# Layer 1's masked-decay products in column tiles of 32 token rows, and the cumulated decays kept in DRAM by steps, in a two-layer GLA and SSD decoder step

## The reference

```python
def ssd_chunk_step(S, inp):
    x, dt, a, Bm, Cm = inp
    c = x.shape[1]
    acum = jnp.cumsum(a, axis=1)
    causal = jnp.tril(jnp.ones((c, c), dtype=bool))[None, :, :, None, None]
    lmat = jnp.exp(jnp.where(causal, acum[:, :, None] - acum[:, None], -jnp.inf))
    cb = jnp.einsum('bign,bjgn->bijg', Cm, Bm)
    y = jnp.einsum('bijg,bijgr,bjgrp->bigrp', cb, lmat * dt[:, None], x)
    y = y + jnp.einsum('bign,bgrpn->bigrp', Cm, S) * jnp.exp(acum)[..., None]
    a_last = acum[:, -1]
    w = jnp.exp(a_last[:, None] - acum) * dt
    S = jnp.exp(a_last)[..., None, None] * S + jnp.einsum('bjgn,bjgr,bjgrp->bgrpn', Bm, w, x)
    return S, y
```

## Time and profile before

| | |
|---|---|
| median of 3 runs | 1575.83 us (1575.52 to 1580.14) |
| the profiled execution | 1581.91 us, of which the trace spans 1580.2 us |
| TensorE, matmuls | 1474.9 us busy, 93% of the span |
| TensorE, weight loads | 1232.4 us busy, 78% (beside the matmuls) |
| VectorE | 1176.9 us, 74% |
| ScalarE | 824.1 us, 52% |
| GpSimd | 252.0 us, 16% |
| mean granted TensorE clock | 0.973 of full speed |
| DMA | 242.92 MB, mean 154 GB/s |

### The profile page before, as it was taken

One profiled execution on the slowest core, in us unless ns is written; L12 is line 12 of the kernel. 1 busy time (PEld: TensorE's weight loads), 2 busy tenths in 40 slices (PEclk: granted clock), 3 DMA queues, 4 the chain that ended last, 5 costly groups with the idle time before them and its releaser, 6 DMA issues. The chain is left out here.

```text
span 1580.2 us, 28320 instructions
## 1 busy us (share of the span) xinstructions
PE 1474.9 (93%) x10074; PEld 1232.4 (78%) x10074; DVE 1176.9 (74%) x2595; ACT 824.1 (52%) x1837; POOL 252.0 (16%) x438
## 2 busy tenths in 40 slices
PE   6989999799999969998999999989989999999985
PEld 5969787567788759898888888867777788888764
DVE  4555587856786887967887898986869787687775
ACT  4735353445556545546665664644646364654451
POOL 5010113001331200111120121210002110000012
PEclk8999999999999999999999999999999999999988
DMA  6455455434576433448855865853675775666641
GB/s 188 134 146 145 138 154 165 119 120 138 145 185 189 141 118 105 142 112 212 236 139 128 234 172 133 232 125 86 194 198 144 177 183 141 171 147 154 163 134 60
DMA packets 312198, 242.92 MB, mean 154 GB/s; under 512 B 32808, under 2 KB 283500, under 8 KB 311900
## 3 DMA queue, kind: packets, MB, share of 16 engines
q1 hardware_dynamic: 302140, 208.28, 48.9%
q0 software_dynamic: 9920, 32.84, 7.7%
HBM read 180.40 MB, written 64.97 MB: 155 GB/s over the span
## 5 line engine op out<-in xcount | busy, mean ns | idle before, releaser
L1439 PE MATMUL bank<-h,w 128*128 128x268 f32 (+1 forms) x4752 | 842.8, 332 | 27.0 <-ACT w L857 21.4
L1439 PEld LDWEIGHTS bank<-h,w 128*128 128x128 f32 x4752 | 706.8, 193 | 104.9 <-issue 33.1
L873 DVE TENSOR_TENSOR w<-w_raw,w 128x1024 fp32r<-128x1024 f32 x132 | 161.0, 1220 | 40.1 <-ACT w L857 39.5
L842 PE MATMUL bank<-s_w_out,s_yt_hi 128*128 128x512 f32 (+2 forms) x544 | 169.7, 402 | 3.2 <-DVE s_ys L2522 2.5
L857 ACT ACTIVATE w<-w_raw 128x1024 fp32r<-128x1024 f32 x132 | 138.7, 1051 | 14.1 <-DMA w_raw<-in_ssd_w_in_dram 14.1
L1517 DVE SCALAR_TENSOR_TENSOR conv<-before_conv,cw,conv 128x260 f32<-128x260 f32 (+2 forms) x216 | 125.3, 580 | 4.2
L842 PEld LDWEIGHTS bank<-s_w_out,s_yt_hi 128*128 128x128 f32 (+2 forms) x544 | 97.1, 182 | 30.5 <-issue 4.2
L842 PE MATMUL bank<-g_w_out,g_ot_hi 128*128 128x512 f32 (+2 forms) x288 | 95.7, 421 | 1.1 <-DVE g_ot_lo L2065 0.9
L842 PE MATMUL bank<-s_w_out,s_yt_lo 128*128 128x512 f32 x240 | 95.6, 398 | 0.0
L2311 ACT ACTIVATE s_decay<-s_decay,t_ac 128x128 f32<-128x128 f32 (+1 forms) x288 | 85.4, 379 | 1.2
L1485 ACT ACTIVATE conv<-bank,cw 128x268 f32<-128x268 f32 (+1 forms) x72 | 45.9, 637 | 75.5 <-PE bank L1439 59.9
(11 more groups left out here) (256 smaller groups left out, 2491.2 us busy)
## 6 DMA issues: line engine op xcount, KB each, us to landing
w_raw<-in_ssd_w_in_dram SPq DMA_DIRECT2D x80, 512.0 KB, 4.2
w_raw<-in_gla_w_in_dram SPq DMA_DIRECT2D x48, 512.0 KB, 4.3
s_decay<-kept_acd SPq DMA_DIRECT2D x32, 512.0 KB, 8.1
w_raw<-in_ssd_w_out_dram SPq DMA_DIRECT2D x30, 512.0 KB, 4.4
g_chunk<-kept_gq SPq DMA_DIRECT2D x32, 448.0 KB, 4.9
s_chunk<-kept_sq SPq DMA_DIRECT2D x32, 384.0 KB, 4.8
kept_sq<-stage SPq DMA_DIRECT2D x80, 134.0 KB, 4.4
kept_sq<-stage SPq DMA_DIRECT2D x40, 256.0 KB, 4.6
```

The source lines that it names most:

```text
L842: last = pe.matmul(bank[0:r, :], yt[a][:, k, 0:r], wo[:, b, 512 * half:512 * half + 512], start=(k + a + b == 0), stop=(k == tiles - 1 and ...
L873: dve.tensor_tensor(self.part(i, 1), self.raw(i), hi, ALU.subtract).then_inc(self.w_lo, 1)
L1439: last = pe.matmul(bank[:, 0:n], w[:, p.tile % 2, a, k, :], h[:, b, k, c:c + n], start=(i == 0), stop=(i == len(terms) - 1))
```

## The change

Three things are edited.

1. In `pe_scan` the product of one head is split over its output's token rows into column tiles of 32: four matmuls with a 128x32 stationary operand, each with its output in another quarter of the PSUM partitions. The moving operand is the same 128x64 slice for all four. Steps of 24 tokens keep one matmul for a head.
2. `kept_acd` is laid out as steps x heads x 128 tokens instead of heads x all tokens. The load of a step's decays reads 8 neighbouring rows of 128, which are 4 KB without a gap, and its DMA is written with 128 rows of 1024 elements instead of 128x8x128.
3. The store of group 0's decays is two DMAs (step 0 with 24 tokens, steps 1 to 4 with 128) instead of one. `all_stored` waits for the higher count.

```diff
-    for name, shape in (("gq", [U, 7 * P, T]), ("sq", [U, 10 * P, T]), ("acd", [SH, T]), ("meta_rows", [NM, D]),
+    for name, shape in (("gq", [U, 7 * P, T]), ("sq", [U, 10 * P, T]), ("acd", [STEPS, SH, P]), ("meta_rows", [NM, D]),
...
     def store(self, sp, G):
         sp.wait_ge(self.scanned, G + 1)
-        c, n = GROUP_COL[G], GROUP_LEN[G]
-        sp.dma_start(self.d["acd"][:, c:c + n], self.room(G)[2]).then_inc(self.stored, 16)
+        ac, q = self.room(G)[2], GROUP_STEPS[G]
+        if G == 0:
+            sp.dma_start(self.d["acd"][0, :, 0:C0], ac[:, 0:C0]).then_inc(self.stored, 16)
+            ac, q = ac[:, C0:], q[1:]
+        sp.dma_start(self.d["acd"][q[0]:q[-1] + 1].rearrange("s h c -> h s c"),
+                     ac.rearrange("h (s c) -> h s c", c=P)).then_inc(self.stored, 16)
+
+    def all_stored(self, engine, G):
+
+        engine.wait_ge(self.stored, 16 * (G + 2))
...
-            sp.wait_ge(self.sizes.stored, 16 * (G + 1))
+            self.sizes.all_stored(sp, G)
...
-        sp.dma_start(self.decay(u, s), d["acd"][HPG * u:HPG * u + HPG, c:c + n].unsqueeze(0).to_broadcast(
+        sp.dma_start(self.decay(u, s), d["acd"][s, HPG * u:HPG * u + HPG, 0:n].unsqueeze(0).to_broadcast(
             [P, HPG, n])).then_inc(self.acb_in[e % 2], 16)
...
         for r in range(HPG):
-            last = pe.matmul(self.Y[0][0:n, r * HD:(r + 1) * HD], G[0:n, r, :], t["xdt"][0:n, r * HD:(r + 1) * HD],
-                             start=True, stop=True)
+            for j in range(0, n, SUB):
+                rows = slice(j, min(j + SUB, n))
+                last = pe.matmul(self.Y[0][rows, r * HD:(r + 1) * HD], G[0:n, r, rows],
+                                 t["xdt"][0:n, r * HD:(r + 1) * HD], start=True, stop=True)
         last.then_inc(self.intra, 1)
...
-            act.wait_ge(self.sizes.stored, 16 * (group_of(s) + 1))
+            self.sizes.all_stored(act, group_of(s))
```

## The result

The changed kernel takes 1552.45 us (median of 4 runs, 1551.42 to 1553.76), the kernel before took 1577.99 us beside it (4 runs, 1575.52 to 1583.47). The ratio is 0.9834, with a 95% interval of 0.9804 to 0.9864: 26 us less, between 21 and 31. The forecast was 15.5 us less and 1560.3 us, its range began at 1554 us. The direction was right; the gain was larger by two thirds, and the time fell out of the range on its fast side.

The account below looks back on a forecast made before the run. TensorE's own stream was taken to bound layer 1. Savings of 14.5 us from the products and 1.0 us from the decays' layout, against the median of 1575.83 us, gave 1560.3 us, with a range of 1554 to 1572 us.

Parts of the forecast that it names:

- TensorE bounds layer 1: In layer 1 time taken off TensorE's own stream comes off the end, as far as VectorE's order and a few waits allow.
- The products after: Layer 1's 64 narrow matmuls a step run side by side, 16 ns apart, 1.02 us a step.
- Layer 0's loss of 11 ns a tile: Time a column tile loses in layer 0; added to the 57 ns stream it gave 17 ns an instruction, 1.09 us a step.
- The change of shape: Switching the array to narrow tiles and back, twice a step around the products, costs 0.17 us for both together.
- The clock: In layer 1 it is at 0.96 to 0.99, nearly always at its upper level: nothing to win, something to lose.
- A step's saving: Each of 32 steps of layer 1's products takes 1.19 us in place of 1.70 us: 0.51 us less, 16.3 us in all.
- What reaches the end: Of the products' saving in layer 1's three stretches, 85%, 95% and 85% come through: 14.5 us.
- The decays' layout: Faster loads of a step's decays, for which only ScalarE waits, give 1 us, with 0 and 5 as bounds.
- The landing: Median time from issue to landing of the decays' load falls from 8.1 us to between 4.4 and 6.
- a worse pace (21 and 24 ns): Two rivals on the products: load and stream in sequence, 1570 us, chance 0.10; a floor on start distances, 1576 us, chance 0.04.
- the slow one: Rival: the products' tiles don't run side by side with the shared moving slice; 3.82 us a step, about 1640 us, chance 0.04.
- More than expected: Rival: ideal pace of the products, and several microseconds from the decays' load: 19.8 + 2 = 22 us, 1554 us, chance 0.06.

## Why the forecast was wrong, step by step

- **TensorE bounds layer 1**: right. The tiles brought 13.8 us alone and 12.6 us on top of the layout by the traces (10 and 12.8 us by the times), with no other change.
- **The products after**: right in mechanism, too careful in pace. The term was 16 ns an instruction, it measured 14.0 ns, the ideal bound. Layer 0's loss of 11 ns a tile did not carry over.
- **The change of shape**: 0.17 us forecast. Entry 0.09 to 0.10 us as forecast, the way out 0.15 us for 0.08 us. Right.
- **The clock**: "nothing to win" was wrong. In the layout's profile TensorE's busy time is 6.4 us less with the same instructions, the clock being at its lower level for 17 us less.
- **A step's saving**: 0.51 us forecast, 0.57 us by the time line and about 0.55 us measured as the shift of later work in a steady stretch, 17.6 us over 32 steps.
- **What reaches the end**: 14.5 of 16.3 us forecast. Measured are 13.8 of 17.6 us (tiles alone) and 12.6 of 17.6 us (on top of the layout). The share was 0.72 to 0.78 instead of 0.89. From step to step between the kernel with the layout alone and the changed one, the whole 0.55 us arrives in the second and third stretch nearly always, while several steps of the first stretch and the last four bring little or nothing, although the forecast let a saving count whole at the end, because the products stood on the chain there. The two errors nearly cancelled: 14.5 us for the tiles came out close, somewhat high, and in part by luck.
- **The decays' layout: here it failed.** The term was 1 us with 5 as its bound, it measured 13.4 us by time and 14.3 us by trace. The step that failed was pricing the load by the sentence that only ScalarE waits for the decays. What stood behind it in the DMA engines, the weights, got one sentence and a part of that 1 us. TensorE waited 12.8 us for weights in layer 1 before and 7.8 us with the layout alone, and it ran on at a lower clock after waits: 7.9 us of idle and 6.4 us of busy time went. The landing of 8.1 us against 4.4 us was read as a matter of packet size; the packets of 512 bytes of other loads took 30 ns on the mean, which would have shown that size could not be it. The bound of 5 us was wrong too: it stayed under ScalarE's 6.4 us.
- **The landing**: 4.4 to 6 us forecast, 6.2 us measured.
- **The rivals** with a worse pace (21 and 24 ns) and the slow one are excluded by the 14.0 ns. "More than expected" was the case that came, with other terms than it named: the pace was ideal, but of its 19.8 us for the tiles 10 to 14 came, and the load gave 13 to 14 us instead of 2. Its reach was 22 us, the measured 26 us.

Not tried: whether the changed kernel gains further from other layouts of `kept_sq`, whose rows are 4192 bytes apart too but are read by one partition each; and rows 4096 or 2048 bytes apart. No version that was run beats the changed kernel.

## What to carry to other kernels

Here a float32 matmul with 64 moving columns and 128 columns of weights was bound by the load (108 ns for a stream of 57); column tiles hid the load and divided the stream, and did so as long as the tiles of one stream stood next to each other in the program. Before pricing a DMA by who waits for its data, look at the GB/s beside its busy share, and at what is queued behind it. When many partitions read the same few rows from DRAM, put the rows next to each other. Distances of 8192, 4192 and 4224 bytes cost time here, 8192 by far the most; a width changed by a few hundred bytes is a cheap trial.

## What the runs showed of the hardware

- Eight rows of 512 bytes read by all 128 partitions: landing 17.2 us at a distance of 8192 bytes, 8.1 at 4192, 7.3 at 4224, 6.7 at 4704, 6.4 at 4608, 6.5 at 544, 6.3 at 640 and 6.2 as one piece of 4 KB. By one number the kernel moved from 1740 to 1567 us. That the rows meet in one part of the memory fits all eight, but it is not shown: where in the memory they meet was not seen. The Trainium skill (DMA: Bandwidth & Descriptors, Latency and other measured facts) tells of slow copies between tensors in DRAM where the rows of the partitions lie 2 to 8 MiB apart, and offers the memory's channels as an unverified reason; the runs here show a loss at 8 KB, for a source that all partitions share. Whether it is the same effect is open.
- Four column tiles in float32 start 14.0 ns apart on the mean with streams of 64 columns, and a tile's next load is hidden behind its stream. With tile outermost, a tile's first matmul started when 3 of the tile before it were left, as far as spacing and length of the records tell. The Trainium skill (TensorE: Matmul & The Clock Gate, The mechanism) says that matmuls start in program order; by the same reading the instructions of the next tile started between the last three of the one before, which speaks against it for column tiles.
- A wait of 4.1 us cost another 2.6 us behind it, 18 instructions of 512 columns taking 7.08 us for 4.44 us, the granted clock being at 0.88 from 1142 to 1170 us.
